# One copy of the attention bias row per head in DRAM, read as a sliding strip, with query order turned inside each tile

## The reference, cut to what matters

```python
def rel_bucket(dist):
    n = jnp.maximum(dist, 0)
    exact = REL_BUCKETS // 2
    ...
    return jnp.where(n < exact, n, large)

logits = q @ k.T * (Dh ** -0.5) + bias[head, rel_bucket(query_pos - key_pos)]
```

## Time and profile before

| | us |
|---|---|
| median of 3 runs | 2799.89 |
| lowest, highest | 2788.68, 2802.16 |
| profiled execution, its own time | 2790.8 |
| its span in the trace | 2788.7 |
| PE busy in the span | 2536.9 |
| DVE, ACT, POOL busy | 849.7, 793.6, 780.8 |

### The profile page before, as it was taken

One profiled execution on the slowest core, in us unless ns is written; L12 is line 12 of the kernel. 1 busy time (PEld: TensorE's weight loads), 2 busy tenths in 40 slices (PEclk: granted clock), 3 DMA queues, 4 the chain that ended last, 5 costly groups with the idle time before them and its releaser, 6 DMA issues.

```text
span 2788.7 us, 38017 instructions
## 1 busy us (share of the span) xinstructions
PE 2536.9 (91%) x16714; PEld 1950.0 (70%) x16714; DVE 849.7 (30%) x1287; ACT 793.6 (28%) x1007; POOL 780.8 (28%) x262
## 2 busy tenths in 40 slices
PE   4998888999999999987989999999799878899998
PEld 3876556777776678345878888888568335678786
DVE  3002336342344541662231111111441553311113
ACT  3122233221223421533232112112432533322222
POOL 1232133333332210410222222222221321344432
PEclk9898799999999999988999999999999778999999
DMA  6541013443343110101111112111110102222221
GB/s 178 140 150 69 17 61 129 155 178 151 151 181 113 55 39 1 45 3 61 61 46 63 58 63 74 58 56 46 70 46 8 45 2 89 78 91 91 91 98 53
DMA packets 42952, 220.52 MB, mean 79 GB/s; under 512 B 4072, under 2 KB 12920, under 8 KB 19492
## 3 DMA queue, kind: packets, MB, share of 16 engines
q1 hardware_dynamic: 35624, 200.52, 19.6%
q10 hardware_dynamic: 7164, 17.57, 2.5%
HBM read 212.05 MB, written 6.03 MB: 78 GB/s over the span
## 4 chain that ended last, share of the span: by engine, by line
PE 75%; DVE 7%; ACT 2%; issue 1%; POOL 0%; DMA 0%; ACTq 0%; DVEq 0%; POOLq 0%
PE PS L654 58%; PE PS L657 2%; PE PS L1051 2%; PE PS L1084 2%; DVE s_states L1449 2%; DVE tmp L587 1%; DVE a_lo L579 1%; PE PS L715 1%; PE PS L1649 1%; PE PS L1757 1%; PE PS L1848 1%; DVE hid_lo L868 1%; PE PS L1101 1%; PE PS L1063 1%; PE PS L537 1%
## 5 line engine op out<-in xcount | busy, mean ns | idle before, releaser
L1966 POOL TENSOR_TENSOR w_lo<-raw,w_hi 128x2048 fp32r<-128x2048 f32 (+2 forms) x146 | 649.7, 4450 | 1653.3 <-ACT w_hi L751 1653.3
L654 PE MATMUL PS<-a_hi,w_hi 128*128 128x512 f32 (+1 forms) x2104 | 694.4, 374 | 88.8 <-DVE a_lo L579 58.3
L654 PE MATMUL PS<-a_lo,w_hi 128*128 128x512 f32 (+1 forms) x2104 | 674.9, 365 | 0.0
L654 PE MATMUL PS<-a_hi,w_lo 128*128 128x512 f32 (+1 forms) x2104 | 673.8, 365 | 0.0
L654 PEld LDWEIGHTS PS<-a_hi,w_hi 128*128 128x128 f32 x2104 | 361.6, 191 | 184.4 <-issue 114.8
L654 PEld LDWEIGHTS PS<-a_lo,w_hi 128*128 128x128 f32 x2104 | 361.2, 191 | 63.3 <-issue 0.7
L654 PEld LDWEIGHTS PS<-a_hi,w_lo 128*128 128x128 f32 x2104 | 359.7, 190 | 65.4
L751 ACT ACTIVATE w_hi<-raw 128x2048 fp32r<-128x2048 f32 (+2 forms) x146 | 270.6, 1853 | 390.6 <-PE PS L654 202.8
L654 PE MATMUL PS<-hid_hi,w_hi 128*128 128x512 f32 (+1 forms) x784 | 265.6, 375 | 29.6 <-DVE hid_lo L868 29.6
L654 PE MATMUL PS<-hid_lo,w_hi 128*128 128x512 f32 (+1 forms) x784 | 263.9, 373 | 0.0
L654 PE MATMUL PS<-hid_hi,w_lo 128*128 128x512 f32 (+1 forms) x784 | 263.7, 373 | 0.0
(11 more groups left out here) (203 smaller groups left out, 2478.9 us busy)
## 6 DMA issues: line engine op xcount, KB each, us to landing
raw<-in_w_ada SPq DMA_DIRECT2D x48, 1024.0 KB, 6.9
raw<-in_w_ff SPq DMA_DIRECT2D x32, 1024.0 KB, 4.7
raw<-in_w_in SPq DMA_DIRECT2D x27, 1024.0 KB, 4.8
raw<-in_w_gate SPq DMA_DIRECT2D x22, 1024.0 KB, 4.7
raw<-in_w_up SPq DMA_DIRECT2D x22, 1024.0 KB, 4.7
raw<-in_w_down SPq DMA_DIRECT2D x16, 1024.0 KB, 4.8
raw<-in_w_out SPq DMA_DIRECT2D x12, 1024.0 KB, 5.6
raw<-in_w_down SPq DMA_DIRECT2D x8, 768.0 KB, 4.2
```

The lines of the kernel that those rows point to most:

```text
L654: mm = p.matmul(ps[:, dst], wv[:, k, idx * P:(idx + 1) * P], av[:, k, dst], start=first, stop=last)
L1966: pool.tensor_tensor(w_lo[:, m % 2, 0:kt, 0:ncol], src, w_hi[:, m % 2, 0:kt, 0:ncol].bitcast(F32), ALU.subtract).then_inc(s_lo.sem, 1)
```

## The change

The table in DRAM becomes one row per head. The DMA that stores it writes 12 rows of 2,560 bytes instead of 1,536. A strip's partition p is now read from number p on, so the source has a step of 1 from partition to partition where it had 639, and the strip comes out with its partitions in reverse order. To fit that, queries are put in reverse order inside each tile of 128 where they lie on partitions: `rounds` reads the queries backwards into `a_hi`, and `diagonal` and the bias product in `turned` use a unit matrix with reversed rows. That matrix is a new constant, loaded by one DMA of 64 KB on ACT's queue right behind the bias rows. PE waits for it once ahead of the first `turned`, POOL once ahead of the first `diagonal`.

```diff
+        turned_ident = over("turned_ident", [P, P], s_at + 14 * K)
-        bias_dram = nc.dram_tensor("bias_dram", [12, P, STRIP], F32)
+        bias_dram = nc.dram_tensor("bias_dram", [12, STRIP], F32)
-                                           rounds=[(a_hi[:, tile, 0:SEQ], proj1[:, qt + pair, :]),
+                                           rounds=[(a_hi[:, tile, 0:SEQ].rearrange("p (i q) -> p i q", q=P),
+                                                    bass.AP(proj1, (qt + pair) * SEQ + P - 1, [[17 * SEQ, P], [P, NX], [-1, P]])),
                                                    (a_lo[:, tile, 0:SEQ], proj1[:, kt_ + pair, :])]))
                 if s == 0 and causal:
+                    p.wait_ge(s_turned_ident.sem, 16)
                     p.wait_ge(S("max").sem, S("max").at(plan["end_unit"][0]))
-                            mm = p.matmul(ps[:, P * i:P * (i + 1)], strips[:, head % 4, P * d:P * (d + 1)], ident[:],
+                            mm = p.matmul(ps[:, P * i:P * (i + 1)], strips[:, head % 4, P * d:P * (d + 1)], turned_ident[:],
                                           start=False, stop=i == NX - 1)
+                if g == 0 and h == 0:
+                    pool.wait_ge(s_turned_ident.sem, 16)
                 pool.tensor_tensor(bdiag1[g % 2][:, h, 0:P * nq].rearrange("p (i q) -> p i q", q=P),
-                                   ident[:].unsqueeze(1).to_broadcast([P, nq, P]),
+                                   turned_ident[:].unsqueeze(1).to_broadcast([P, nq, P]),
-                src = bass.AP(bias_dram, head * P * STRIP + P - 1, [[STRIP - 1, P], [1, SEQ]])
+                src = bass.AP(bias_dram, head * STRIP, [[1, P], [1, SEQ]])
                 a.dma_start(strips[:, head % 4, :], src).then_inc(S("strip").sem, 16)
-            act.dma_start(bias_dram[:, :, :], bias_row[:].unsqueeze(1).to_broadcast([12, P, STRIP])).then_inc(s_load_bias.sem, 16)
+            act.dma_start(bias_dram[:, :], bias_row[:]).then_inc(s_load_bias.sem, 16)
+            act.dma_start(turned_ident[:], dram["turned_ident"]).then_inc(s_turned_ident.sem, 16)
     c = {"ident": np.eye(P, dtype=f)}
+    c["turned_ident"] = np.eye(P, dtype=f)[::-1]
```

More of the change, by code:

```diff
@@ L1273, in blocks_kernel @@
         s_load_bias = sem("bias_rows_stored")
+        s_turned_ident = sem("turned_ident_loaded")
         class Scan:
```

## The result

The changed kernel took 2768.65 us in the median of 5 runs (2751.09 to 2781.22), the kernel before 2795.68 in the median of now 5 (2788.68 to 2802.16). The ratio is 0.9897, with a 95% interval of 0.985 to 0.9944: 1.0% faster. The forecast was 2764, with 2748 to 2783.

What follows compares the result with a forecast made beforehand. PE, busy 91% of the span, loses time only where it stands still or runs below full clock, behind the slow bias store; 17.4 us of waiting and 13.6 of clock, 31.0 off 2795, give 2764 (2748 to 2783 for 8 in 10).

Steps and rivals of the forecast that it cites:

- The store as cause, and the byte count: Windows of 40 to 122 us: 11.86 MB less 7.87 MB of panel loads leaves 3.99 MB, the bias store, delaying early panels.
- Each panel issued behind it shares them: Early in1: the slow bias store fills the DMA engines, 72% busy at 83 GB/s, and later-issued panels share them.
- Five periods worth 31.0 us: in1, panel 2 to panel 6: savings of 14.1, 2.1, 0, 13.9 and 0.9 us, together 31.0 us.
- Waits 17.4, clock 13.6: Split of the 31.0 us gained in in1: 17.4 us of PE waiting and 13.6 us of lost clock.
- Panel 2 rounded 4.7 us after its issue, spare at least 0.9: Panels 2 to 5 load like panel 6; 11.3 us with hand-overs fits each preceding panel, smallest spare 0.9 us at panel 5.
- New load, two waits, other unit matrix, reversed reads, strips: Side effects of the change, each taken as 0; far bounds +3.0 us for reversed reads and +21 for strips.
- Rival B: Strips, read from single DRAM rows, come slower; gain shrinks to between 25 and 10 us, 2770 to 2785; chance 0.11.
- Rival C: PE's waits in in1 go but the clock doesn't come back; only 17.4 us gained, 2778; chance 0.05.
- D: The store isn't what delays the panels, or only for its first 10 us; gain 0 to 9, 2786 to 2795; chance 0.05.
- E: Slower: strip reads of one DRAM row served one after another; up to 550 us extra, kernel 3310; chance 0.03.
- Everything behind shifts as a block: Stages behind panel 6 start earlier by the full 31.0 us and take as long as now, as in1's end is an engine meeting.
- The baseline: Time of the kernel before, taken as 2795, the mean of four times (2788.7, 2790.8, 2799.9, 2802.2).

Runs made afterwards that it cites:

- e1: Changed kernel with the old store (128 copies of each of the 12 rows, read by nobody) put beside the new one; ratio 0.9989 to the kernel before.
- e3: Changed kernel with an added unread store of 32 copies of each row (0.98 MB) beside the new one; ratio 0.9937 to the kernel before.
- e4b: Kernel before, with useless matmuls (64 ahead of panel 2, 20 ahead of panel 4) into a half bank no panel uses; ratio 0.9925 to the kernel before.
- e8: Changed kernel, unaltered, timed and traced again; 2764.4 us against 2791.5 for the kernel before, ratio 0.9907.
- e7: Changed kernel with the ada panel behind main panel 8 put behind panel 12; median 2763.8 us, ratio 0.99 to the kernel before.
- e5: Changed kernel with one more 1 MB DMA at the end of in1, four heads' strips from the single rows; traced once, landed in 5.3 us.
- e2: Changed kernel with the 12 stored rows also copied 128 times from DRAM to DRAM by 16 engines (3.93 MB, unread); ratio 0.9946 to the kernel before.

## Why the prediction was right, point by point

- **The store as cause, and the byte count:** right, and shown by e1. The end of the store, put after 95 us, is between 93 and 94. The fit of 2 us plus bytes at 436 GB/s (the Trainium skill, "DMA: Bandwidth & Descriptors", Anatomy of one DMA) is given there for DMAs issued by GpSimd; this store is issued by ACT, so the 55 us from its issue at 38.5 to its end don't contradict the page.
- **"Each panel issued behind it shares them":** too mild. From 42 to 53 us only a quarter of panel 2 and its `ada` panel passed (the rows of the queues at e3), 0.52 of the 1.36 MB that moved.
- **Five periods worth 31.0 us:** measured 30.9. The issues came at 42.2, 54.7, 67.2, 80.3, 92.5 and 105.0 for 41.5, 54.0, 66.4, 79.5, 91.7 and 104.2: all about 0.8 us late, because the first panel ended that much later, an offset that was there ahead of panel 2. Ahead of the first maximum another 1.8 us were gained that the sum had not, 1.2 of them in panel 9, whose period from issue to issue was 19.8 us (167.73 to 187.52) and is 18.6 (137.56 to 156.15). In all 31.9.
- **Waits 17.4, clock 13.6:** the split holds as a sum of rows, but the parts aren't free of each other. With the clock alone mended (e4b) 9.6 us come, because the later loads then are the ones that are waited for. The 13.6 us also hold panel 4's long stay at half clock, for which no reason is shown.
- **Panel 2 rounded 4.7 us after its issue, spare at least 0.9:** 4.9 for panel 2, 5.3 for panel 3, which still fits. The smallest spare, at panel 5, held in the first trace, with 0.5 us of waiting there in e8 and 0.7 in e7.
- **New load, two waits, other unit matrix, reversed reads, strips:** 0 each, as taken, as far as the 0.4 us between e1 and the kernel before can tell for `in1`. The load landed in 1.8 us, and L1225 takes 0.624 us for 0.626. **Rival B** is worth 0.4 us per DMA, and DVE's wait for strips isn't longer for it.
- **Rival C** fell with the windows, **D** with e1, **E** with e5.
- **"Everything behind shifts as a block":** the step that failed. It was to carry the gain of `in1` (31.0 us forecast, 31.9 measured) to the end, and 22.2 us arrived in the profiled pair and 26.2 in e8. In the profiled pair 2.65 of the missing 9.7 us are in the attention stage, by its clock; the rest lies behind and is within the spread of what the same stages took in the other kernels. The prediction's range left room for the clock in later stages; the forecast itself put it at nothing. That the median of the timed runs came within 5 us of 2764 is partly luck, since these stages vary by more than that. The timed gains, 27 and 27 us by the difference of medians, with intervals from 16 to 42 and 20 to 32 us, hold 31 and 22 alike. Whether a few microseconds are lost for good stays open.
- **The baseline:** 2795 was taken from four times; the median of five runs is 2795.68. Taking the median of the first three alone, 2799.9, would have given 2769, by chance the number measured.

## What to carry to other kernels

Count the bytes in the windows around a hole in PE: what is left after all the loads that you can name is the transfer that nobody waits for, and it may be the one that costs. A side transfer needn't be waited for to be on the path; here it cost twice, 17.4 us by lateness and 13.6 us by the clock that fell while PE stood still. Not issuing it was best; a form that uses all engines and is soon over took away more than half of the loss (e2). Issuing the old store later, when no panel is due soon, was not tried. And a gain read off one stage arrives at the end only up to the spread of the clock in the stages behind it.

## What the runs showed of the hardware

- A store of 3.93 MB out of 12 partitions kept the DMA engines 72% busy at 83 GB/s, each row of 2,560 bytes 0.38 us on its engine; the same bytes copied from DRAM to DRAM with 128 as outermost dimension, in pieces of 30,720 bytes, landed 16.6 us after the issue, with loads beside them. A rule of the Trainium skill ("DMA: Bandwidth & Descriptors", Rules for kernel authors) fits the first with its bound of c engines for an outermost dimension of c. It can't explain it all: 12 of 16 engines would be a loss of a quarter, and each engine ran at 6.8 GB/s where e2's ran at 21.
- A load issued behind a slow store on another queue needn't get half of the engines' time: from 42 to 53 us 0.52 MB of panels passed beside 0.84 MB of store. With 0.98 MB of store ahead of it, a panel that lands in 4.9 us took 16.1; on the same queue, behind 3.93 MB, a load of 64 KB took 54.7 us for 1.8.
- At half clock, a panel of 128-column products kept PE busy for 22.8 us and the granted clock didn't rise; it was back during the next panel, of 512-column products (mean 0.94 from 122 to 136 us). When PE hadn't stood still (e4b), the same panel ran at 1.00 all through.
- Overlapping reads, 128 out of each 2.5 KB row of DRAM, landed about 0.4 us later than the same reads from rows of their own, both for 256 KB (3.3 to 3.4 us for 2.9 to 3.0) and for 1 MB (5.3 us for 4.9).
